# Two moves just ahead of a mixture of experts: the slot numbers turned before the residual's whole move, and the memory's sums, root and reciprocal inside the output projection

## What is computed

```python
x = x + merged @ w_o[l]
h = rmsnorm(x, g_ffn[l])
aff = jax.nn.softmax((h @ w_router[l]).astype(f32), axis=-1)
vals, idx = lax.top_k(jnp.swapaxes(aff, 1, 2), cap)     # cap = 32 of 256 tokens for each expert
xe = h[bidx, idx]
gt = jnp.einsum('becd,edf->becf', xe, w_gate[l])
up = jnp.einsum('becd,edf->becf', xe, w_up[l])
ye = jnp.einsum('becf,efd->becd', jax.nn.silu(gt) * up, w_down[l])
x = x + jnp.zeros_like(x).at[bidx, idx].add(ye * vals)
...
# second block, in each of two layers
rms_norm(mem, norm_mem[l])                              # mem: 256 rows of 1024
```

## Time and profile before

| | |
|---|---|
| median of three runs | 2585.06 us |
| lowest and highest of them | 2584.26 and 2587.38 us |
| the profiled execution's own time | 2582.32 us |
| its span, first to last instruction | 2580.4 us |
| PE busy | 2292.9 us (89%) |
| DVE busy | 1070.6 us (41%) |
| ACT busy | 855.1 us (33%) |
| POOL busy | 79.5 us (3%) |
| granted TensorE clock, mean over the span | 0.94 |

### The profile page before, as it was taken

One profiled execution on the slowest core, in us unless ns is written; L12 is line 12 of the kernel. 1 busy time (PEld: TensorE's weight loads), 2 busy tenths in 40 slices (PEclk: granted clock), 3 DMA queues, 4 the chain that ended last, 5 costly groups with the idle time before them and its releaser, 6 DMA issues.

```text
span 2580.4 us, 37341 instructions
## 1 busy us (share of the span) xinstructions
PE 2292.9 (89%) x15324; PEld 1634.5 (63%) x15324; DVE 1070.6 (41%) x1681; ACT 855.1 (33%) x1348; POOL 79.5 (3%) x87
## 2 busy tenths in 40 slices
PE   7999998777777777777779999999999999999999
PEld 7996593233333322233237889788888889878887
DVE  7868860000000000000015557756455547666554
ACT  4483141001000100000015445545445445545543
POOL 0000012000000000000000000100000000200000
PEclk9999999878888888888889999999999999999999
DMA  6534089999999999999996544043556554123553
GB/s 245 179 131 152 4 356 405 427 427 427 428 427 427 427 427 427 427 428 426 427 387 204 195 165 170 19 169 126 194 182 207 193 184 167 67 101 130 181 194 114
DMA packets 116822, 669.21 MB, mean 259 GB/s; under 512 B 10826, under 2 KB 14069, under 8 KB 56400
## 3 DMA queue, kind: packets, MB, share of 16 engines
q1 hardware_dynamic: 111376, 650.14, 64.7%
q0 software_dynamic: 3008, 12.96, 1.4%
q10 hardware_dynamic: 2304, 4.20, 0.4%
HBM read 662.01 MB, written 5.24 MB: 259 GB/s over the span
## 4 chain that ended last, share of the span: by engine, by line
PE 59%; DMA 25%; DVE 4%; SPq 4%; issue 3%; ACT 2%; DVEq 1%; POOLq 1%; POOL 0%; ACTq 0%
PE psd L698 22%; PE psd L692 10%; PE psx L698 9%; DMA hx<-in_w_down 7%; DMA ring<-in_w_down 7%; DMA scr<-in_w_up 7%; SPq L3229 4%; PE psx L1131 2%; PE psd L1114 2%; PE psd L1072 1%; PE psx L1386 1%; PE psd L1062 1%; DMA e_w_lo<-in_w_up 1%; DMA e_w_hi<-in_w_up 1%; PE psx L942 1%
## 5 line engine op out<-in xcount | busy, mean ns | idle before, releaser
L2238 DVE TENSOR_TENSOR w_lo<-ring,w_hi 128x1024 fp32r<-128x1024 f32 x436 | 515.6, 1220 | 391.0 <-ACT w_hi L1661 389.7
L1661 ACT ACTIVATE w_hi<-ring 128x1024 fp32r<-128x1024 f32 x436 | 437.2, 1048 | 479.4 <-PE psd L698 253.7
L698 PE MATMUL psd<-w_hi,h_cut 128*128 128x512 f32 x1536 | 481.5, 395 | 5.9 <-DVE w_lo L2238 2.3
L692 PE MATMUL psd<-h_cut,w_hi 128*128 128x256 f32 x1824 | 336.0, 286 | 12.0 <-DVE h_cut L2238 7.8
L698 PEld LDWEIGHTS psd<-w_hi,h_cut 128*128 128x128 f32 x1536 | 284.2, 188 | 63.9 <-DVE w_lo L2238 2.7
L698 PE MATMUL psd<-w_lo,h_cut 128*128 128x512 f32 x768 | 300.5, 391 | 0.0
L692 PEld LDWEIGHTS psd<-h_cut,w_hi 128*128 128x128 f32 x1824 | 286.8, 194 | 16.9 <-issue 14.2
L692 PE MATMUL psd<-h_cut,w_lo 128*128 128x256 f32 x912 | 259.5, 285 | 0.0
L1650 ACT ACTIVATE scr<-psd 128x512 f32<-128x512 f32 (+1 forms) x54 | 30.9, 573 | 566.7 <-PE psd L1088 359.2
L698 PE MATMUL psx<-w_hi,halves 128*128 128x512 f32 x704 | 218.0, 391 | 0.0
L2238 DVE TENSOR_TENSOR scr<-psd,scr 128x512 f32<-128x512 f32 (+1 forms) x24 | 15.9, 668 | 437.6 <-PE psd L1072 436.3
(11 more groups left out here) (416 smaller groups left out, 2900.6 us busy)
## 6 DMA issues: line engine op xcount, KB each, us to landing
ring<-in_ffn_wi SPq DMA_DIRECT2D x88, 1024.0 KB, 5.7
scr<-in_w_gate SPq DMA_DIRECT2D x48, 1024.0 KB, 26.6
scr<-in_w_down SPq DMA_DIRECT2D x48, 1024.0 KB, 26.2
scr<-in_w_up SPq DMA_DIRECT2D x48, 1024.0 KB, 26.7
ring<-in_ffn_wo SPq DMA_DIRECT2D x44, 1024.0 KB, 4.9
ring<-in_w_gate SPq DMA_DIRECT2D x32, 1024.0 KB, 26.8
ring<-in_w_up SPq DMA_DIRECT2D x32, 1024.0 KB, 27.0
ring<-in_w_down SPq DMA_DIRECT2D x32, 1024.0 KB, 26.5
```

What stands on the lines that cost most here:

```text
L692: mm = pe.matmul(o, w[u], a[:, v, :], start=start and i == 0, stop=stop and i == 2, **kw)
L698: mm = pe.matmul(o, a[:, u, :], w[v], start=start and i == 0, stop=stop and i == 2)
L1661: act.activation(hi, src, ACT.Copy).then_inc(hi_cut, 1)
L2238: return dve.tensor_tensor(o, a, b, op)
```

## The change

PE's program, as the diff has it:

```diff
             for i in range(4):
+                if i == 3:
+                    b = XB.claim(pe, ("mem_sum",))
+                    pe.wait_ge(S("mem_squared"), 1)
+                    for n in range(2):
+                        mm = pe.matmul(b[:, 0:T], ones, mem_sq[:, 0, n, :], start=(n == 0), stop=(n == 1))
+                    mm.then_inc(S("mem_summed"), 1)
                 dense(("w_o", i), mn_cut, ready=None if i else ("merged", 0),
...
+            def warm_up(n):
+
+                for _ in range(n):
+                    pe.matmul(psd[0][:, :], ident, con[:, 0:512], start=True, stop=True)
+
             token_rows(0)
             for i in range(4):
                 DB.claim(pe, ("moe", i))
+            warm_up(1)
             pe.wait_ge(S("aff"), 1)
...
             mm.then_inc(S("aff_turned"), 1)
-            pe.wait_ge(S("mem_squared"), 1)
-            for i in range(2):
-                mm = pe.matmul(psd[1][:, 0:T], ones, mem_sq[:, 0, i, :], start=(i == 0), stop=(i == 1))
-            mm.then_inc(S("mem_summed"), 1)
             token_rows(1)
...
-            move_x(range(2))
+            warm_up(1)
             pe.wait_ge(S("slotT"), 1)
...
             mm.then_inc(S("slots_turned"), 1)
-            move_x(range(2, 4)).then_inc(S("x_moved"), 1)
-            pe.wait_ge(S("mem_rooted"), 1)
+            move_x(range(4)).then_inc(S("x_moved"), 1)
```

ACT, DVE and POOL:

```diff
                 if i == 2:
-                    act.activation(tiny[:, 8:9], eps_col, ACT.Sqrt)
+                    act.wait_ge(S("mem_summed"), 1)
+                    act.activation(rmem, XB.bank(("mem_sum",))[:, 0:T], ACT.Sqrt, bias=eps_col,
+                                   scale=1.0 / D).then_inc(S("mem_rooted"), 1)
...
-            act.wait_ge(S("mem_summed"), 1)
-            act.activation(rmem, psd[1][:, 0:T], ACT.Sqrt, bias=eps_col, scale=1.0 / D).then_inc(S("mem_rooted"), 1)
...
+                if i == 2:
+                    dve.wait_ge(S("mem_rooted"), 1)
+                    dve.reciprocal(rmem, rmem).then_inc(S("mem_root"), 1)
...
-            dve.wait_ge(S("mem_rooted"), 1)
-            dve.reciprocal(rmem, rmem).then_inc(S("mem_root"), 1)
...
             pool.wait_ge(S("mem_root"), 1)
+            pool.wait_ge(S("xs_ready"), 1)
             pool.tensor_tensor(mem, mem, rmem.unsqueeze(1).broadcast_to([P, KD, T]), ALU.mult)
```

More of the change, by code:

```diff
@@ L288, in small_plan @@
     add("dve", "router")
+    add(None, "mem_sum")
     for tt in range(TT):
@@ L454, in program @@
         DB = Banks(dense_plan(), psd, d_read)
-        XB = Banks(small_plan(), psx, x_read, [(which, l, 3) for l in range(LAYERS) for which in ("ffn1", "ffn2")])
+        XB = Banks(small_plan(), psx, x_read, [("mem_sum",)] + [(which, l, 3) for l in range(LAYERS) for which in ("ffn1", "ffn2")])
         def slot_of(key):
```

## The result

Twenty-two runs of each kernel, beside each other: before, median 2585.45 us (2581.47 to 2588.16); changed, median 2587.82 us (2585.71 to 2594.11). The ratio of the means is 1.0014, 95% interval 1.0007 to 1.0020: slower by 3.6 us (1.8 to 5.2), which is clear of zero and lies inside the 0.2% that I had called no change. The medians lie 2.4 us apart. The profiled execution of the changed kernel took 2587.11 us, its span 2585.3.

A forecast was written before the change was run, and what follows sets the result against it. The expert stage was taken as bound by transfers, its start by PE's queue. Terms 0.90 - 0.20 - 0.97 + 1.89 - 0.10 = +1.52 us on the median 2585.06 gave 2586.6 us, range 2583.2 to 2590.0.

The forecast's parts named there:

- sums in the projection: Four instructions for the memory's sums ahead of piece 3 in the output projection, on the path: +0.90 us, at most 1.92.
- `aff` turned: PE's turn of `aff` ahead of DVE's top-k gets faster if the first `warm_up` holds the clock up: -0.20 us.
- turn earlier: The slot numbers' turn on PE could start at 381.82 rather than 382.79, if PE is free: -0.97 us.
- `move_x` behind it: Sixteen `move_x` instructions that filled PE's wait now stand between the slot numbers' turn and the gather: +1.89 us.
- copy, and issue: DVE's copy behind the gather no longer comes right behind the reciprocal: -0.10 us, between 0 and -0.12.
- The end hangs on the start of the wide products: At the experts' start: later wide products start the transfer stream later, and nothing in it gives the time back.
- Root and reciprocal: Moved into the projection, ACT's root and DVE's reciprocal have 3.4 us of cover in DVE's wait: 0.
- POOL's new wait: POOL starts 1.8 us later and delays the memory's keys and next refill, with nearly 13 us of cover: 0.
- a sign of being right: Clock of 1.00 at PE's turn of `aff`, listed among the things that would show the prediction right.
- the clock falls under the turn and `move_x`: Rival: 3 us of half clock on PE add 1.5 us, +3.0 in all, 2588.1 us; chance 0.15.

The follow-up runs named there:

- the other arrangement: Kernel before with the memory's sums in PE's wait for `aff`, three quarters of `move_x` ahead of the turn, reciprocal and larger `onehot` later: ratios 0.9993 and 0.9994.

## Why the prediction was right, and where it was not

No change beyond 0.2% was forecast and none came, and the time lies in the range; the loss was under-sized, +1.5 forecast against +3.6 (1.8 to 5.2). By its terms, as differences between starts in the rows of before and in the two profiles of the changed kernel:

| term | forecast | first profile | again |
|---|---|---|---|
| sums in the projection (addition 2 to addition 3, 7.53 before) | +0.90 | +0.86 | +0.86 |
| `aff` turned (addition 3 to first `max`, 6.12 before) | -0.20 | +0.19 | +0.94 |
| turn earlier (first `max` to the turn, 6.83 before) | -0.97 | -1.06 | -1.06 |
| `move_x` behind it (turn to gather, 2.11 before) | +1.89 | +1.79 | +3.42 |
| copy, and issue (gather to refill, 3.68 before) | -0.10 | -0.08 | -0.08 |
| sum | +1.52 | +1.70 | +4.08 |

**What held.** The end hangs on the start of the wide products: 20.4 us in the stretch gave 19.1 in the time. The sums cost what four instructions of 256 columns cost, because the projection binds (0.86 in every profile that has them there). Root and reciprocal are hidden. The turn comes a microsecond earlier and gains nothing, since the sixteen instructions that had filled PE's wait now follow it. The sum books that microsecond to the new order of `move_x`; the runs show that either move alone gives it (0.97 with `move_x` moved, 1.06 with the sums moved) and both together give it once, so beside the sums' move the new order had nothing to gain. POOL's new wait is covered.

**What failed: the two terms that rest on the clock.** The step on `aff`'s turn said that the first `warm_up` fits the 1.14 us for which PE waited and makes the turn faster. It fits at full clock (0.90). But the clock falls near that very place, as it did before (0.50 from 375 to 378): in the four profiles of the changed order it reads 0.73, 0.57, 0.71 and 0.53 there, where the prediction had named 1.00 as a sign of being right. So the warm-up takes 1.47 to 1.92 us, `aff`'s turn waits for it, and the term is +0.19 to +1.01 instead of -0.20 (the 1.01 in part by the router's logits, at half clock too). And the rival "the clock falls under the turn and `move_x`" had 0.15 of the chance; in three of four profiles the clock falls under `move_x`, with 3.38 to 3.42 instead of 1.89 for that term. Its price of 1.5 us for the half clock was right (5.47 - 3.84 = 1.63). I had taken the second `warm_up` as a reason against it, though PE stands idle 1.60 to 1.91 us between it and the turn in those three. With that rival as the likeliest case the forecast would have been its 2588.1, against 2587.82 measured; that the two are so near is in part luck, since the kernel before measured 0.4 higher beside it and `aff`'s term stays wrong in the rival too.

The Trainium skill (Perfetto Trace Analysis, section Matmul Optimizations) says that the matmul engine scales its power with its use, and that matmuls should be issued back to back. The rows agree in part: the clock stays at 1.00 in both profiles of the arrangement whose sums fill the wait for `aff`, and reads 0.52 under `move_x` where PE had waited 1.11 and 1.83 us. But the first `warm_up` follows the token rows without a pause and ran below full clock in all four profiles, and in the first of them `move_x` ran at full clock behind waits of 0.97 and 1.22 us. Why the sums held the clock where the warm-up in the same place did not stays open.

**How the sizes meet.** The four stretches of the changed order average 29.7 us, the two of before 26.6: 3.1 us, inside the interval of 1.8 to 5.2. The rest of the 4.9 us between the first two profiles lies outside the stretch. Ahead of it (1.33 us) the repeats had piece 2 at 362.2, so that part belongs to the execution. Behind it, from the first refill to the end of the span, before took 2191.8 and 2189.6 us and the changed kernel 2193.7 and 2193.9, but the other arrangement alone gave 2197.1 and 2190.6 in its two profiles, so two against two tell nothing there. Whether a part of the 3.6 beyond 3.1 is more than chance stays open.

## What to carry to other kernels

When a wait is filled by work that is needed later anyway and that ends before the wait does, the work isn't in the way: moving it behind the wait brings nothing forward and lengthens the path by the whole of the work. Ask which engine's queue binds just ahead of the next stage, and leave on it only what that stage can't start without. Filler that is to keep the clock up had better be work that counts, as the sums were in the last arrangement, and it must fit the wait at half clock too: the warm-up that fitted at 0.90 us took up to 1.92. And price a stretch of small products at both clocks before choosing one: several profiles of the same kernel here differ by 2.4 us in 30.

## What the runs showed of the hardware

The clock's falls move from one execution to the next: the same program had a stretch of 27.97 us and one of 30.35, 1.63 us of the difference by `move_x` at 3.84 and at 5.47 us, the other 0.75 by `aff`'s turn.

In the other arrangement DVE's larger comparisons (128x448) met POOL's multiplication, and the second of them lasted until it was done. DVE and POOL there:

```profile
386.49 5.42 DVE L2239 TENSOR_TENSOR scr<-con,scr 128x448 f32<-128x448 f32 x2
```

```profile
386.65 4.78 POOL L3161 TENSOR_TENSOR scr<-scr 128x2048 f32<-128x2048 f32 x1 [31.64 <-DVE scr L2725]
```

The two comparisons took 5.42 us, 4.94 of it the second, which started behind POOL's start and ended 0.5 us behind its end (386.65 + 4.78 = 391.43); before, these two and the two small ones took 1.64 together. DVE's next copy to `xs` was late and PE waited 2.00 us for it, behind the first refill, where the queue of transfers covered it. The Trainium skill (SBUF — State Buffer, section Who interferes with whom) says that a DVE instruction with two inputs in SBUF contends with a GpSimd instruction that reads SBUF, that the ports they share are an exclusive lock, and that the order of issue decides which of two blocks; the rows agree. The changed kernel's wait for `xs_ready` would keep such a meeting away from the top-k, but no run here leaves that wait out.
